# Query products of heads 2 and 3 moved in between the first expert sums, and their routing drawn together

## The reference, cut to what matters

```python
x = x + gate1[:, None, :] * (merged @ w_out[l])
h2 = modulate(rmsnorm(x, norm2_g[l]), shift2, scale2)
x = x + gate2[:, None, :] * peer(h2, peer_wq[l], peer_subkeys[l], peer_u[l], peer_v[l])

def peer(h, wq, subkeys, u_tab, v_tab):
    q = (xt @ wq).reshape(T, PEER_HEADS, 2, PEER_HALF)             # 8 heads, 2 halves of 128
    sc = jnp.einsum('thpd,hpkd->thpk', q, subkeys)                 # 128 keys for each half
    vals, ids = lax.top_k(sc, PEER_TOPK)                           # 16 best of each half
    cand = vals[:, :, 0, :, None] + vals[:, :, 1, None, :]         # 256 sums for a head
    top, pos = lax.top_k(cand, PEER_TOPK)                          # 16 experts for a head
    idx = ...                                                      # id0 * 128 + id1 at pos
    g = jax.nn.softmax(top, axis=-1)
    a = jnp.einsum('chkd,cd->chk', jnp.take(u_tab, idx, axis=0), xt)
    out = jnp.einsum('chk,chkd->cd', g * jax.nn.gelu(a), jnp.take(v_tab, idx, axis=0))
```

## Time and profile before

| | us |
|---|---|
| median of 3 runs | 1365.8 (1365.75 to 1366.97) |
| the profiled execution | 1365.89 |
| its span | 1364.2 |
| PE busy | 1222.4 (90%) |
| DVE busy | 866.4 (64%) |
| POOL busy | 519.8 (38%) |
| ACT busy | 425.0 (31%) |
| sums on PE (L987), 1024 instructions | 499.3 |
| dots on DVE (L2114), 256 instructions | 312.1 |

### The profile page before, as it was taken

One profiled execution on the slowest core, in us unless ns is written; L12 is line 12 of the kernel. 1 busy time (PEld: TensorE's weight loads), 2 busy tenths in 40 slices (PEclk: granted clock), 3 DMA queues, 4 the chain that ended last, 5 costly groups with the idle time before them and its releaser, 6 DMA issues.

```text
span 1364.2 us, 14254 instructions
## 1 busy us (share of the span) xinstructions
PE 1222.4 (90%) x4539; PEld 642.5 (47%) x4539; DVE 866.4 (64%) x1726; ACT 425.0 (31%) x1126; POOL 519.8 (38%) x578
## 2 busy tenths in 40 slices
PE   7999979999877877777898787899999999999997
PEld 2676545665322222223453222663444445999443
DVE  2446378574575766777667678478997343677335
ACT  2212244333443443443434434322116111222000
POOL 1000057765777777777777777002111000000000
PEclk9999989999999999999999999999999899999999
DMA  9897599999999999999999999363333344354450
GB/s 348 300 329 275 191 350 391 409 391 405 404 410 409 409 409 409 410 409 409 408 409 406 408 407 403 120 246 123 124 123 124 108 159 167 137 184 148 167 182 31
DMA packets 130794, 397.32 MB, mean 291 GB/s; under 512 B 10380, under 2 KB 11788, under 8 KB 130463
## 3 DMA queue, kind: packets, MB, share of 16 engines
q0 software_dynamic: 74448, 271.09, 50.3%
q1 hardware_dynamic: 54404, 120.14, 24.5%
q10 hardware_dynamic: 1868, 5.18, 1.1%
HBM read 395.32 MB, written 1.05 MB: 291 GB/s over the span
## 4 chain that ended last, share of the span: by engine, by line
PE 47%; DMA 24%; POOL 10%; DVE 9%; issue 5%; DVEq 3%; ACT 1%; POOLq 0%; ACTq 0%
DMA gathered<-in_peer_u_dram,expert_idx 18%; PE psum L675 18%; PE psum L1269 6%; PE psum L1308 6%; PE psum L987 6%; POOL gathered L584 5%; POOL gathered L598 5%; DMA gathered<-in_peer_v_dram,expert_idx 4%; DVE work L1769 3%; DMA weight_ring<-in_w_in_dram 2%; DVE gathered L2114 2%; DVE work L2401 2%; PE psum L783 2%; PE psum L702 1%; PE psum L757 1%
## 5 line engine op out<-in xcount | busy, mean ns | idle before, releaser
L987 PE MATMUL psum<-gathered,modr 128*128 128x512 f32 x1024 | 499.3, 618 | 112.0 <-DMA gathered<-in_peer_v_dram,expert_idx 94.3
L2114 DVE CUSTOM_DVE_ANT_0 gathered<-gathered,psum 128x1024 f32<-128x1024 f32 x256 | 312.1, 1219 | 176.5 <-DMA gathered<-in_peer_u_dram,expert_idx 175.3
L987 PEld LDWEIGHTS psum<-gathered,modr 128*128 128x128 f32 x1024 | 180.3, 192 | 408.8 <-DMA gathered<-in_peer_v_dram,expert_idx 242.5
L584 POOL DMA_INDIRECT gathered<-in_peer_u_dram,expert_idx x256 | 249.4, 974 | 255.2 <-DVE expert_idx L1777 166.7
L598 POOL DMA_INDIRECT gathered<-in_peer_v_dram,expert_idx x256 | 241.3, 942 | 101.1 <-issue 70.0
L675 PE MATMUL psum<-weight_ring,featT 128*128 128x512 f32 x384 | 171.2, 600 | 1.7 <-ACT featT L1360 1.7
L1524 ACT ACTIVATE gel<-dots 128x1 f32<-128x1 f32 x256 | 51.5, 201 | 279.3 <-DVEq L2116 279.1
L1769 DVE TENSOR_TENSOR work<-work 128x1088 f32<-128x1088 f32 (+4 forms) x107 | 99.9, 950 | 26.8 <-ACT work L1622 18.7
L675 PEld LDWEIGHTS psum<-weight_ring,featT 128*128 128x128 f32 x384 | 71.5, 191 | 91.8 <-issue 89.6
L675 PE MATMUL psum<-featT,weight_ring 128*128 128x128 f32 (+2 forms) x768 | 107.7, 297 | 4.5 <-DVE work L1769 1.9
L675 PEld LDWEIGHTS psum<-featT,weight_ring 128*128 128x128 f32 x768 | 100.5, 191 | 20.5 <-issue 11.8
(11 more groups left out here) (365 smaller groups left out, 1372.0 us busy)
## 6 DMA issues: line engine op xcount, KB each, us to landing
weight_ring<-in_w_in_dram SPq DMA_DIRECT2D x13, 2048.0 KB, 9.1
weight_ring<-in_ada_w_dram SPq DMA_DIRECT2D x9, 2048.0 KB, 17.3
weight_ring<-in_w_up_dram SPq DMA_DIRECT2D x8, 2048.0 KB, 8.2
weight_ring<-in_w_down_dram SPq DMA_DIRECT2D x8, 2048.0 KB, 7.8
gathered<-in_ada_w_dram SPq DMA_DIRECT2D x3, 2048.0 KB, 13.3
weight_ring<-in_peer_wq_dram SPq DMA_DIRECT2D x3, 2048.0 KB, 12.0
gathered<-in_w_in_dram SPq DMA_DIRECT2D x2, 2048.0 KB, 13.5
gathered<-in_peer_u_dram,expert_idx POOLq DMA_INDIRECT x256, 11.0
```

What stands on the lines that cost most here:

```text
L584: pool.indirect_dma_start(u_rows[:, slot, :], None, T["peer_u"], bass.IndirectOffsetOnAxis(ap=expert_idx[:, r % 2, k:k + 1], axis=0),).the ...
L987: mm = pe.matmul(psum[:, SUM_BANK + half, :], diag[:, e % 8, :], v_rows[:, slot, 512 * half:512 * (half + 1)], start=(e % EXPERTS == 0), s ...
L2114: dve.tensor_tensor_reduce(u_rows[:, slot, :], u_rows[:, slot, :], h2_rows[t], 1.0, 0.0, ALU.mult, ALU.add, dots[:, col:col + 1])
```

## The change

The products `wqa` 4 to 7 leave their place between `ada(11)` and `ada(10)`; one of them now stands behind each of sums 0 to 3, in banks 0 and 1 as the sums hold 2 and 3. Their scores, `score_step(1, 0)`, stand behind sum 5. On ACT the copies follow: one behind each of the weighings of experts 1 to 4, the root of tile 1 behind the one of expert 3, the copy of the scores behind the one of expert 6. On DVE the first four pieces of head 1's routing stand ahead of dot 0, so that the others end with dot 8; the routing of heads 2 and 3 begins with dot 9 instead of 6 and has two pieces for each dot, so that it ends with dot 19 instead of 27. Its exponent on ACT moves from step 18 to 16.

```diff
+WQA_AT = {0: 4, 1: 5, 2: 6, 3: 7}
+SCORE_1_AT, SCORE_1_READ, ROOT_1_AT = 5, 6, 3
+AHEAD = 4
...
+NARROW.update({("wqa", _i): (0, 1) for _i in range(4, 8)})
...
             ada(11)
-            for a in range(4, 8):
-                by_feature("wqa", a, wq_w[1], a % 4, 0, P)
             ada(10)
-            for a in range(4, 8):
-                read_wait(pe, "wqa", a)
-            score_step(1, 0)
...
                 sum_expert(e)
+                if e in WQA_AT:
+                    a = WQA_AT[e]
+                    by_feature("wqa", a, wq_w[1], a % 4, 0, P)
+                if e == SCORE_1_AT:
+                    for a in range(4, 8):
+                        read_wait(pe, "wqa", a)
+                    score_step(1, 0)
...
             read_turn(gate_parts[11], turn_bank("ada", 11, 0), "ada", 11, 0)
-            for a in range(4, 8):
-                read_queries("wqa", a, 0)
             read_turn(gate_parts[10], turn_bank("ada", 10, 0), "ada", 10, 0)
-            read_scores(1, 0)
-            act.wait_ge(flag("x1_ready"), 2)
-            row_root(xres[:, 1, :], 1, junk_n2, D, "n2_sd")
...
                 weigh_expert(e)
+                if e - 1 in WQA_AT:
+                    read_queries("wqa", WQA_AT[e - 1], 0)
+                if e == ROOT_1_AT:
+                    act.wait_ge(flag("x1_ready"), 2)
+                    row_root(xres[:, 1, :], 1, junk_n2, D, "n2_sd")
+                if e == SCORE_1_READ:
+                    read_scores(1, 0)
...
-                if e == 18:
+                if e == 16:
                     softmax_exp(2)
...
-            ROUTE_PIECES, FIRST_NEXT = 22, 6
+            ROUTE_PIECES, FIRST_NEXT = 22, 9
...
-                if e < ROUTE_PIECES // 2:
-                    route_piece(1, 2 * e)
+                if e < (ROUTE_PIECES - AHEAD) // 2:
+                    route_piece(1, AHEAD + 2 * e)
                     dve.drain()
-                    route_piece(1, 2 * e + 1)
-                if 0 <= e - FIRST_NEXT < ROUTE_PIECES:
-                    dve.drain()
-                    route_piece(2, e - FIRST_NEXT)
+                    route_piece(1, AHEAD + 2 * e + 1)
+                if 0 <= e - FIRST_NEXT < ROUTE_PIECES // 2:
+                    for i in range(2):
+                        dve.drain()
+                        route_piece(2, 2 * (e - FIRST_NEXT) + i)
...
             residual(1, 0)
+            for i in range(AHEAD):
+                dve.drain()
+                route_piece(1, i)
```

## The result

The changed kernel is slower: 1376.07 us (median of 6 runs) against 1365.68 us (median of 6 runs of the kernel before on the same chip), a ratio of 1.008 with a 95% interval of 1.0065 to 1.0095. That is 10.4 us; the prediction had 4.5 us and a range up to 1373.0 us. The profiled execution of the changed kernel took 1377.57 us (span 1375.8).

The account below looks back on a forecast made before the run. The 512 gathers bound the kernel from mid-phase on, so early DMA shortage is never won back. Sum 15 5.0 us late less 0.5 us from the queue gave + 4.5 us: 1370.3 us, range 1363.5 to 1373 us.

Parts of the forecast that it names:

- The start of sum 15 less 229.6 us: PE, expert phase: this shift is the price of the change; sum 15 predicted at 234.6 us, 5.0 us late.
- Both waits of DVE: DVE waits for ACT: 5.9 us behind dot 5 for the root, 2.1 us behind dot 7 for head 1's exponent.
- v gather 3: POOL: goes out in its turn at 185.0 us, its wait of 4.27 us for ada(10) gone.
- that sum 0 runs at the lower level and costs 3.4 us in place of 1.7: PE after its rests around ada(10): only sum 0 meets the 1.2 GHz clock, at 3.4 us instead of 1.7.
- the far end: PE clock: ada(10) slow as well as sum 0, costing about 3.6 us; the other end was no fall, 0.
- reciprocal behind dot 5: DVE: ready for it at 196.6 us, waits 5.9 us until ACT's root is done at 202.5 us.
- reduction of piece 19: DVE behind dot 7: there at 209.6 us, waits 2.1 us for head 1's exponent on ACT at 211.7 us.
- From sum 15 PE is continuous again: PE from sum 15 on has no pause, so the shift reaches the second place where DMA lacked work unchanged.
- the queue: DMA queue at the second place, 280 to 290 us: faster landings give back 0.5 us, at most 2.1 us.
- The faster case: Rival: ACT's root ready by 196.6 us, DVE never waits, sum 15 3.1 us early: 1362.7 us; chance 0.2.
- The worse case: Rival: ada(10) at the lower clock too, root 2 us later still: + 6.5 us, 1372.3 us; chance 0.15.
- The other rule that was weighed: ACT: 2.66 us per table switch, adding some 1.4 us at each of three switches; sum near 8.7 us.

Follow-up runs that it names:

- half_wq: Changed kernel with 8 of the 16 matmuls left out of each of the products `wq` 8 and `wq` 9: 1370.85 us, ratio 1.0041 to the kernel before.
- after_warm: Changed kernel plus 16 and 10 unread products of the identity ahead of and behind ada(10): ratio 1.0045 to the kernel before, + 5.4 us.
- exp2_17: As both_early, with the exponent of heads 2 and 3 behind weighing 17 instead of 16: ratio 1.0021 to the kernel before, + 2.7 us.
- both_early: Changed kernel with ACT's root behind the second weighing and head 1's exponent behind the third: ratio 1.002 to the kernel before, + 2.9 us.
- both_warm_2: both_early plus 16 and 10 unread identity products ahead of and behind ada(10), on a 409 GB/s chip: ratio 0.9988 to the kernel before, - 2.1 us.
- swap_ahead_2: Kernel before with four head 1 pieces ahead of dot 0 and ada(10) ahead of `wqa` 7, on a 409 GB/s chip: ratio 0.9985, - 2.2 us.
- warm: Changed kernel plus 36 and 20 unread products of the identity ahead of and behind ada(10): ratio 1.0063 to the kernel before, + 8.6 us.
- both_single_2: both_early with heads 2 and 3 routed one piece a dot, their exponent behind weighing 22, on a 409 GB/s chip: ratio 1.0032 to the kernel before.

## Why the prediction went wrong

**What was right.** The sign, the mechanism and where it sits. The start of sum 15 less 229.6 us was named as the price; it is 240.17, or 9.6 us with the 1.0 us of the later start taken off, and half_wq shows in its trace that PE carries such a shift one to one. Both waits of DVE are where they were put. v gather 3 waits 1.12 us. What the DMA gained before 205 us (v gather 8 lands 3.4 us sooner) was lost to waits for dots.

**The step that failed is the clock, a term mis-sized and a place overlooked.** The text took "that sum 0 runs at the lower level and costs 3.4 us in place of 1.7", and gave "ada(10) slow as well" a place as the far end. Measured, with the 1.0 us taken off:

| | predicted | measured | further late |
|---|---|---|---|
| ada(10) | 1.94 us long | 3.67 | 1.7 |
| `wqa` 4 | 1.8 | 2.7 from start to start | 0.9 |
| reciprocal behind dot 5 | 202.5 | 205.1 | 2.6 so far |
| sums 4 and 5 | 3.5 | 5.2 to the scores | 1.8 |
| reduction of piece 19 | 211.7 | 216.1 | 4.4 so far |
| dot 12 | 223.4 | 227.9 | 4.5 |
| dot 15 | 232.1 | 236.7 | 4.6 |
| sum 15 | 234.6 | 239.2 | 4.6 |

Each later number is off by what the clock cost beyond the 1.7 us foreseen, at most 4.4 us, and by 0.2 us besides that I can't place. The lower clock thus costs 6.1 us in the changed kernel (1.7 for each of ada(10) and sum 0, 0.9 and 1.8), of which the sum had 1.7. It costs that much because ACT, and by ACT DVE, waits for each product of this stretch: the root stands behind `wqa` 6. after_warm shows the cost: it takes away 4.3 of the 6.1 us and is 5.0 us faster. That the waiting reader is the reason is read from the order of the rows. The second rest of after_warm agrees with it, for the fall there, where PE had 1.40 us to wait, cost nothing.

The far end deserved more than a place at the edge. The trace of before had one row of a rest with the clock's fall behind it, a rest of 5.85 us. I called a rest of 4.6 us open and left ada(10) out of the sum. The rest was 4.70 us, and the granted clock from the start of ada(10) to its end was 0.50. The Trainium skill (TensorE: Matmul & The Clock Gate, section HAM oscillation) had said that a burst behind each rest can start cold. This trace agrees, with 3.67 us for ada(10) and 3.75 us for sum 0, though the sums behind its rest of 2.05 us at 217 us ran at full speed. The place overlooked is sums 4 and 5: the prediction had PE wait there for the root's table loads, and didn't ask what this rest does to the clock.

**Two small steps.** "From sum 15 PE is continuous again" isn't so: it waits 0.83 us ahead of sum 17, for softmax_exp(2), which the change moved to step 16 and which the prediction didn't cost at all; `wq` 8 is 11.7 us late where sum 15 was 10.6. exp2_17 shows that one step later gains nothing. And the queue gave back 0.1 us (`wq` 8 late by 11.72, the last dot by 11.59) where 0.5 was taken.

**The sum again**, for the start of the last dot: 5.0 as predicted + 4.4 for the clock + 0.2 not placed + 1.1 between sum 15 and `wq` 8, with the exponent - 0.1 for the queue + 1.0 for the later start = 11.6 us, measured 11.59. Without the later start it is 10.6, against 10.4 us between the medians.

**The rivals.** The faster case needed ACT's root by 196.6 us; both_early gives that (no wait behind dot 5), and then the scores were the next wait, so it was still slower. Only with the clock kept up as well, in both_warm_2, is the median below the kernel before, by 2.1 us, and its interval (0.9976 to 1.0001) just includes no change. The worse case, with ada(10) slow, was the right one and had 0.15; it too lacked sums 4 and 5 and the exponent.

**What stays open.** Why the interval of swap_ahead_2 points to 2 us where its trace shows 0.5 us. What decides whether a rest of 2 us is followed by the lower clock: the same rest was in some kernels and not in others. And how much of the delay of sums 4 and 5 is the rest of 2.03 us itself and how much the clock behind it; no run was made to part them, but in warm, where the rest stayed and the clock held, they took 1.7 us less. Whether the two pieces behind each dot could be undone without the loss at sum 23.

The other rule that was weighed, 2.66 us for a switch of tables (ScalarE: Activation LUTs, section What ACT_TABLE_LOAD costs, in the Trainium skill), would have given 8.7 us and so have been nearer, but not by its reason: the loads at 215.52 us and elsewhere took 1.28 us and the next activation followed 0.02 us behind.

## What to carry to other kernels

When an edit makes PE wait between short products, price each of the products up to the next long run of work at the lower clock, not only the first one, and again at each later wait that the edit adds, as the worse end of the range: here a rest of 2 us brought it in six cases of ten. Then ask who stands behind them: a slow product costs nothing where its reader is late (the second fall of after_warm), and its whole length where a serial engine, here ACT, is queued on it.

A shift that is made at the start of a long saturated phase is best read at the last place where the engine that paces it has slack, here the start of `wq` 8; that one start gave the last dot to 0.5 us in ten kernels of thirteen. In the other three PE gained or lost time behind it, and one of them, both_single_2, is a warning: moving a table load on ACT to another step can make PE wait there.

When the profile names a releaser, ask of the kernel's source whether the engine waits for it at all. The wait of v(29) was put down to a dot for which no v gather waits.
